# Index dots of a sparse attention front: the second key block between the dots, all query tiles behind them

## The reference, cut to what matters

```python
c_q, k, v, k_idx, w_idx = jnp.split(proj, [R, R + H*d, R + 2*H*d, R + 2*H*d + DI], axis=-1)
c_q = rms_norm_2(c_q, cq_g)
q = (c_q @ w_uq).reshape(B, S, H, d)
q_idx = apply_partial_rope((c_q @ w_uq_idx).reshape(B, S, HI, DI), cos, sin)
k_idx = apply_partial_rope(rms_norm_2(k_idx)[:, :, None, :], cos, sin)[:, :, 0]
...
dots = jnp.einsum('bqhe,bke->bqhk', qib, k_idx)
score = jnp.einsum('bqh,bqhk->bqk', wb, jax.nn.relu(dots))
score = jnp.where(mask, score, -jnp.inf)
vals, idx = lax.top_k(score, topk)
```

## Time and profile before

| | before |
|---|---|
| median of 3 runs | 2361.71 us (2361.28 to 2361.82) |
| profiled execution | 2358.69 us |
| its span | 2356.9 us |
| TensorE matmul busy | 2323.0 us (99%) |
| ScalarE, VectorE, GpSimd busy | 851.7, 789.6, 1178.8 us |
| stretch from the first dot to the products behind the dots | 1776.44 to 1800.31 us |

### The profile page before, as it was taken

One profiled execution on the slowest core, in us unless ns is written; L12 is line 12 of the kernel. 1 busy time (PEld: TensorE's weight loads), 2 busy tenths in 40 slices (PEclk: granted clock), 3 DMA queues, 4 the chain that ended last, 5 costly groups with the idle time before them and its releaser, 6 DMA issues.

```text
span 2356.9 us, 26928 instructions
## 1 busy us (share of the span) xinstructions
PE 2323.0 (99%) x11114; PEld 1887.0 (80%) x11114; DVE 789.6 (34%) x1368; ACT 851.7 (36%) x1258; POOL 1178.8 (50%) x982
## 2 busy tenths in 40 slices
PE   8999999999999999999999999999999999999999
PEld 7888887888977888888887678888887757788887
DVE  3222204864223312201457642022046853310310
ACT  4222214514343322212446543123156464431330
POOL 6544445636555544454452364444556944544442
PEclk9999999999999999999999999999999999999999
DMA  4332323212332322323220123233231202323322
GB/s 149 102 96 90 107 90 110 90 60 84 125 107 72 105 92 94 103 90 107 72 90 19 54 90 106 91 92 105 90 103 59 85 1 72 90 90 102 95 90 90
DMA packets 147585, 209.61 MB, mean 89 GB/s; under 512 B 7260, under 2 KB 113927, under 8 KB 147463
## 3 DMA queue, kind: packets, MB, share of 16 engines
q1 hardware_dynamic: 147462, 207.89, 27.4%
HBM read 205.77 MB, written 2.10 MB: 88 GB/s over the span
## 4 chain that ended last, share of the span: by engine, by line
PE 86%; DVE 7%; POOL 2%; issue 2%; ACT 1%; DMA 1%; SPq 0%; DVEq 0%; POOLq 0%; ACTq 0%
PE ps L1530 27%; PE ps L1532 26%; PE ps L1531 26%; DVE c_work L3049 1%; POOL wlo L794 1%; DVE c_best L3048 1%; DVE small L2892 1%; DVE hl L2465 1%; PE ps L2325 1%; PE ps L2306 1%; POOL sq L809 1%; PE ps L1869 1%; PE ps L1891 1%; PE ps L2296 1%; DMA raw<-in_mlp_w 0%
## 5 line engine op out<-in xcount | busy, mean ns | idle before, releaser
L794 POOL TENSOR_TENSOR wlo<-raw,whi 128x512 fp32r<-128x512 f32 x772 | 1001.6, 1329 | 987.1 <-ACT whi L1014 963.0
L1014 ACT ACTIVATE whi<-raw 128x2048 fp32r<-128x2048 f32 x184 | 350.5, 1905 | 675.6 <-DMA raw<-in_mlp_w 314.7
L1530 PE MATMUL ps<-hh,whi 128*128 128x512 f32 x1448 | 571.8, 395 | 7.1 <-DVE hl L2465 5.7
L1531 PE MATMUL ps<-hl,whi 128*128 128x512 f32 x1448 | 565.0, 390 | 0.0
L1532 PE MATMUL ps<-hh,wlo 128*128 128x512 f32 x1448 | 564.9, 390 | 0.0
L1530 PEld LDWEIGHTS ps<-hh,whi 128*128 128x128 f32 x1448 | 272.6, 188 | 73.0 <-issue 9.4
L1532 PEld LDWEIGHTS ps<-hh,wlo 128*128 128x128 f32 x1448 | 272.4, 188 | 57.1
L1531 PEld LDWEIGHTS ps<-hl,whi 128*128 128x128 f32 x1448 | 272.8, 188 | 56.5 <-issue 1.2
L1530 PE MATMUL ps<-gh,whi 128*128 128x512 f32 x736 | 286.4, 389 | 0.0
L1531 PE MATMUL ps<-gl,whi 128*128 128x512 f32 x736 | 286.4, 389 | 0.0
L1532 PE MATMUL ps<-gh,wlo 128*128 128x512 f32 x736 | 286.4, 389 | 0.0
(11 more groups left out here) (451 smaller groups left out, 2861.8 us busy)
## 6 DMA issues: line engine op xcount, KB each, us to landing
raw<-in_mlp_w SPq DMA_DIRECT2D x64, 1024.0 KB, 5.3
raw<-in_ffn_w_up SPq DMA_DIRECT2D x22, 1024.0 KB, 5.1
raw<-in_ffn_w_down SPq DMA_DIRECT2D x22, 1024.0 KB, 4.8
raw<-in_ffn_w_gate SPq DMA_DIRECT2D x21, 1024.0 KB, 5.2
raw<-in_w_in SPq DMA_DIRECT2D x12, 1024.0 KB, 5.1
raw<-in_diff_w_in SPq DMA_DIRECT2D x12, 1024.0 KB, 5.1
raw<-in_xattn_w_kv SPq DMA_DIRECT2D x8, 1024.0 KB, 5.0
raw<-in_dsa_w_in SPq DMA_DIRECT2D x8, 1024.0 KB, 4.9
```

The costliest lines, as they stand in the source:

```text
L794: nc.gpsimd.tensor_tensor(wlo[i][:, c], raw[i][:, c], whi[i][:, c].bitcast(F32), ALU.subtract).then_inc(s_lo, 1)
L1014: nc.scalar.activation(whi[i][:, 0:width(made[0])], raw[i][:, 0:width(made[0])], ACT.Copy)\
L1530: nc.tensor.matmul(dst, w_hi, x_hi, start=start, stop=False)
L1531: nc.tensor.matmul(dst, w_hi, x_lo, start=False, stop=False)
```

## The change

The order of the blocks and of TensorE's work is altered. The first half of the K1 weights is loaded as b+5, the query weights as b+6, the second half of K1 as b+7. K0 tile 3 is made ahead of all dots, in place of the two query tiles there. No product stands between dots 8 to 15. Behind each of dots 16 to 31 one `mm3` of the first half of K1 is made, 3 products, 16 times. Each of dots 9 to 11 waits for its own bank's transposes' copy only. All eight query tiles come behind the dots, on banks 0 to 3 in place of 4 to 7, Q0 waiting for the last four scores, Q1 for the copies of Q0. ScalarE's copies of the query tiles, and the squares, move behind the last relu; the small root of Q1 goes behind the copies of K1. VectorE makes 8 rounds of tile 1 before the first head sum and 8 between the first and the second (before: 1, none, 15). GpSimd rotates the Q0 rows ahead of the low part of block b+11, where it did so behind it.

```diff
-K_STEP, Q_STEPS = 9, (11, 14, 17, 20, 24, 28)
+K_STEP, K1_FROM = 9, 16
@@ SyncE
-                    load(b + 5, cols_of(wdram["dsa_w_uq_2"]))
-                    b += 6
-                    for c0 in (768, 1280, 1792):
+                    load(b + 5, wide_src(w, 768)(0))
+                    load(b + 6, cols_of(wdram["dsa_w_uq_2"]))
+                    load(b + 7, wide_src(w, 768)(1))
+                    b += 8
+                    for c0 in (1280, 1792):
@@ GpSimd
                 scaled(1, c_rowb, "dsa_q_norm_2", b + 9)
+                split_to(b + 10)
+                rotated(1, c_rowb)
                 split_to(b + 11)
-                rotated(1, c_rowb)
@@ ScalarE
-                    bank = 4 + st if group != G_IQ else st
+                    bank = st if group in (G_IQ, G_Q0, G_Q1) else 4 + st
...
-                for st in range(2):
-                    put_rows(G_Q0, st, c_rowb[:, st, :], None, c_n[:, st:st + 1])
...
-                    if v in Q_STEPS:
-                        g, st = divmod(2 + Q_STEPS.index(v), ST)
-                        if g == 0:
-                            put_rows(G_Q0, st, c_rowb[:, st, :], None, c_n[:, st:st + 1])
-                        else:
-                            put_rows(G_Q1, st, c_rowc[:, st, :], None, c_n[:, st:st + 1])
...
-                for group, rows, squares in ((G_Q0, c_rowb, c_sq0), (G_Q1, c_rowc, c_sq1)):
-                    act.wait_ge(s_cc, dsa_copied(group, ST - 1))
-                    nc.scalar.activation(squares[:, :, :], rows[:, :, :], ACT.Square).then_inc(s_csq, 1)
+                for st in range(ST):
+                    put_rows(G_Q0, st, c_rowb[:, st, :], None, c_n[:, st:st + 1])
+                act.wait_ge(s_cc, dsa_copied(G_Q0, ST - 1))
+                nc.scalar.activation(c_sq0[:, :, :], c_rowb[:, :, :], ACT.Square).then_inc(s_csq, 1)
+                for st in range(ST):
+                    put_rows(G_Q1, st, c_rowc[:, st, :], None, c_n[:, st:st + 1])
+                act.wait_ge(s_cc, dsa_copied(G_Q1, ST - 1))
+                nc.scalar.activation(c_sq1[:, :, :], c_rowc[:, :, :], ACT.Square).then_inc(s_csq, 1)
                 prep_to(b + 8)
@@ TensorE
-                use(b + 5)
-                for st in range(2):
-                    copied(G_K0, st)
-                    full(compressed(b + 5, 0, 1024, st, 4 + st), G_Q0, st)
+                full(rows_half(b + 4, 1, 3, 7), G_K0, 3)
+
+                def second_keys(i):
+
+                    st, k = divmod(i, 4)
+                    if i == 0:
+                        use(b + 5)
+                    if k == 0:
+                        copied(G_K0, st)
+                    w = (b + 5) % NBUF
+                    r = mm3(ps[:, 4 + st, :], hh[:, k, ts(st, P)], hl[:, k, ts(st, P)], whi[w][:, ts(k, S)],
+                            wlo[w][:, ts(k, S)], k == 0, False)
+                    if i == 15:
+                        r.then_inc(s_used, 1)
...
-                    if v == K_STEP:
-                        full(rows_half(b + 4, 1, 3, 7), G_K0, 3)
-                    if v in Q_STEPS:
-                        g, st = divmod(2 + Q_STEPS.index(v), ST)
-                        copied(G_Q0 if g else G_K0, st)
-                        full(compressed(b + 5, 512 * g, 1024, st, 4 + st), (G_Q0, G_Q1)[g], st)
+                    if v >= K1_FROM:
+                        second_keys(v - K1_FROM)
                 use(b + 6)
                 for st in range(ST):
-                    copied(G_Q1, st)
-                    r = rows_half(b + 6, 0, st, 4 + st)
-                r.then_inc(s_used, 1)
+                    pe.wait_ge(s_cacc, 29 + st - IH)
+                    full(compressed(b + 6, 0, 1024, st, st), G_Q0, st)
+                for st in range(ST):
+                    copied(G_Q0, st)
+                    full(compressed(b + 6, 512, 1024, st, st), G_Q1, st)
@@ VectorE
-                top(1, 0, 1)
+                top(1, 0, 8)
                 stats(1, c_sq0, G_Q0)
+                top(1, 8)
                 stats(2, c_sq1, G_Q1)
-                top(1, 1)
```

## The result

The changed kernel takes 2395.14 us (median of 4 runs, 2394.49 to 2396.08) against 2361.49 us before (4 runs, 2360.17 to 2361.82): 1.0145 times as long, interval 1.0132 to 1.0158, or 33.7 us more. 2371.2 was forecast, with a range of 2366 to 2375. The direction was right; the size was not. Executions of one kernel differ by some 4 us with their mean granted clock (before, over all sessions: 2357.1 to 2358.1 us at 1.000, 2359.3 to 2362.1 at 0.998), so one or two microseconds between medians say little.

A forecast was written before the change was run, and what follows sets the result against it. TensorE, busy 2323.0 of 2356.9 us, was taken as the bound, with VectorE's selection tying the loop's start. Dots' stretch +10.8 us, less 1.3 given back, made +9.5 on 2361.7: 2371.2, range 2366 to 2375.

The forecast's parts named there:

- The first dot and dots 8 to 15: First dot stays at 1776.44; the eight dots without products between them take 5.4 us, bounds 4.5 to 6.5.
- A lone dot as dear as a pair: Dots 16 to 31: a dot without partner costs 0.84 us at 384 keys and 1.06 at 512, like a first pair.
- 0.20 fixed in each lump: Products between dots: each lump costs a fixed 0.20 us plus 0.23 a product, so three cost 0.89.
- first rival: Dots 16 to 31: lone dot costs only its streaming, lumps have no fixed part; +3.1 us, 2364.8; chance 0.09.
- second rival: Dots 16 to 31: products hide behind the dots; steps under 0.9 us, 2354.8, faster; chance 0.04.
- The sum without the clock: From the dots to the query products +10.8 us; for the whole kernel net +9.5 us.
- What is given back: Start of the attention loop: VectorE stands 1.8 us earlier against TensorE; 1.3 us regained, bounds 0 to 1.8.
- The other edits at nothing: Query tiles' bank waits, head sums, load order and GpSimd's rotation order: each costs nothing.
- Block b+8: Weight block behind the second K1 half: ready at 20.6, wanted at about 23.5, margin 2.9 us; coming late had chance 0.04.
- rival 3: Behind dots 8 to 15 the clock falls to 0.50 for three microseconds, about 1.6 us more; 2372.8; chance 0.10.

The follow-up runs named there:

- experiment 2: The changed kernel with its 16 groups of 3 products behind dots 12 to 27 instead of 16 to 31: 2370.51 us, ratio 1.0042.
- experiment 3: The changed kernel plus one spare group of 3 products behind each of dots 11 to 14: 2372.92 us, ratio 1.0047.
- experiment 7: The changed kernel with K0 tile 3's 12 products behind dot 9 again: six executions with mean 2395.0 us, four with mean 2370.4; ratio 1.0105.
- Experiment 1: The changed kernel with its 48 products dealt out in the old lumps, 12 behind dot 9, then six of 6: 2361.39 us, ratio 1.0003.
- experiment 6: The changed kernel with 12 products behind dot 24, 3 behind each of dots 16 to 23 and 28 to 31: 2379.87 us, ratio 1.0085.
- experiment 4: The changed kernel with, from dot 16 on, two dots together and then 6 products, 8 times: 2365.18 us, ratio 1.0021.
- experiment 5: The changed kernel with 12 products together behind dot 16 and 3 behind each of dots 20 to 31: 2371.27 us, ratio 1.0046.

## Why the prediction was wrong, and where it was right

- **The first dot and dots 8 to 15.** Forecast 5.4 us up to dot 16; 5.34 in the trace (1776.91 to 1782.25). Right.
- **A lone dot as dear as a pair; 0.20 fixed in each lump.** Forecast 0.84 and 1.06, 0.89 for the three products, steps of 1.73 and 1.95. Measured at full clock 0.84 and 1.05, 0.89, 1.73 and 1.94. Right, which refutes the first rival (0.64 and 0.85). The second rival, products hidden behind dots, falls with it, since no step comes under 0.9 us. The drain at a change of tiling mode that the Trainium skill states (TensorEngine Tiling (Array Packing), Key Properties) fits these steps; no run separates a drain from another fixed cost.
- **The sum without the clock.** Up to the query products +10.8 us was forecast; in the change they come 35.2 later, and without the 24.5 of the clock over the lone dots that is 10.7. For the whole, +9.5 was forecast. With the clock held, experiment 2, which has two pairs more at the end, is at 0.42% or 9.9 us (forecast for it 2369, measured 2370.5), experiment 3 with its twelve spare products at 0.47% or 11.1 (forecast 2374, measured 2372.9), and the four high-clock executions of experiment 7 lie around 2370.4. Two slips of the working changed nothing: the stated bounds add up to 2376 at the upper end, not 2374; and the first rival took 0.40 off each of 16 steps, 6.4 us, which is not the 3.2 of eight more changes of mode.
- **What is given back.** VectorE was to end its scores 0.5 behind the query products' start and the loop was to gain 1.3. In experiment 3 VectorE's last score and its first work for the attention are these:

```profile
1811.13 0.75 DVE L3042 SCALAR_TENSOR_TENSOR c_score<-ps,small,c_score 128x512 f32<-128x512 f32 x1 [1.20 <-ACT ps L1428]
...
1878.10 0.29 DVE L3079 CUSTOM_DVE_ANT_0 c_s<-ps,c_bias 128x128 f32<-128x128 f32 x1
```

  The score ends at 1811.88, 0.67 behind 1811.21, and VectorE reaches the attention 66.9 behind the products, where before took 1869.66 - 1800.31 = 69.4: 2.5 earlier. But the loop's first turned inverse, before and in experiment 3, shows how little of it arrives:

```profile
1883.06 0.41 PE L2338 MATMUL ps<-ident,c_inv 128*128 128x128 f32 x2 [0.57 <-ACT a_qT L1030]
```

```profile
1893.41 0.41 PE L2346 MATMUL ps<-ident,c_inv 128*128 128x128 f32 x2 [0.56 <-ACT a_qT L1025]
```

  82.75 against 82.20 behind the products: 0.55 given back, not 1.3. TensorE's idle time in the loop did not shrink, though VectorE came 2.5 us earlier: 2.38 us between 1866.70 and 1883.06 before, 2.46 between 1877.40 and 1893.41 in experiment 3. The rows above wait for ScalarE's copy `a_qT`, not for VectorE. The forecast had put only 0.5 of the 1.8 idle microseconds down to such copies; the term was 0.8 too large.
- **The other edits at nothing.** Experiment 1 bears it out for all of them together. Block b+8 came in time: TensorE is busy without a gap from 1840 to 1900.
- **The step that failed: rival 3.** Its trigger was the right one: thin dots 8 to 15 bring the clock down. What it had wrong is how long the clock stays down. Its size was 1.6 us and its chance 0.10; measured, 24.5 us over the lone dots and 1.8 over the first query products; the mean clock of 0.987 or 0.988 says that all four executions fell alike. The size came from the earlier trace rows, where after a pause of TensorE the clock was at 0.50 for about 3 us. What stood behind that pause were products without a break. Here lone dots with three products stood behind it, and on those the clock does not come back: it stayed at 0.50 for 58 us in the change and 31 in experiment 6, until dense products came. The chance was too low as well: the argument against it, no gap over 1 us, and a loop that idles 1.8 of 13.3 us at 1.00, took gaps as what matters; the stretch fell with its longest gap under 1 us too, at 3.48 busy of 5.00. The Trainium skill (TensorE: Matmul & The Clock Gate, What's actually happening) ties the clock to how busy TensorE has recently been; the trace agrees for the fall, but for the rise the busy time of the profile is no guide, since it shows TensorE busy throughout at 0.50.

What stays open: why lone dots with three products do not bring the clock up, while groups of two dots with six products do (experiment 4). Two things differ there: the products take 1.38 of every 2.42 us in place of 0.69 of 1.73, and two dots run at a time in place of one. No run separates them. Also open is how thin a stretch must be: in experiment 7 the same stretch goes either way. In the change all four executions fell, and four are few to call that certain.

## What to carry to other kernels

Work taken out of a stretch in which TensorE waits for other engines may cost more than its own time: the clock can fall there, and what comes behind decides how long it stays down. Look at the granted clock of every stretch that a change thins out, and at the first dense run of matmuls behind it; twelve spare matmuls in the thin stretch (22 us), or a lump of real ones directly behind it (24 us), won most of the loss back here. Twelve products as one lump behind the second of the thin dots were not enough in six of ten executions (experiment 7). And price small row-tiled matmuls by groups: one alone costs what two on the array's two halves cost (0.84 and 1.05 us in experiment 3; the pairs of experiment 4 take 0.85 and 1.06), and of each visit some 0.4 us, by the differences of the rows, is fixed.

## What the runs showed of the hardware

- TensorE shown busy 18.00 of 18.00 us at a granted clock of 0.50: full busy time is no sign of full clock; a stretch's count of matmuls, beside that of a like stretch, is (30 in 18 us against 98 in 20 us, though the mix differs).
- The clock stayed where it was over lone 64-row dots with three 128x512 products behind each: at 0.50 for 58 us in the change, at 1.00 behind the lump in experiment 5 for 23.5 us, and over all sixteen such steps in experiments 2 and 3.
- A stretch between the change's thin one and a filled one made one program bimodal: 2370.4 or 2395.0 us in experiment 7, with nothing between.
- One 64-row fp32 dot (two matmuls in the trace) among full-height products takes 0.84 us at 384 and 1.05 at 512 columns; with its three products 1.73 and 1.94 at 1.00, 3.15 and 3.58 at 0.50.
